# Two-layer attention and FFN trunk on one core: output projection accumulated head by head inside attention, probabilities scaled on the pool engine

## The reference

```python
# layer 0: 8 NSA heads, each with a compressed, a selected and a window branch, and 8 MLA heads
s = q @ k.T * scale + bias                 # per head and branch, causal
p = softmax(s)
o = gate_c * (p_c @ v_c) + gate_s * (p_s @ v_s) + gate_w * (p_w @ v_w)     # NSA
o = softmax(qn @ kn.T + qr @ kr.T) @ v                                      # MLA
x = x + gate * (concat(o, all 16 heads) @ w_out)                            # 2048 x 2048
# layer 1: 16 DSA heads, keys picked per token by an indexer's top 64
x = x + gate * (concat(o, 16 heads) @ w_out)
```

## Time and profile before

| what | value |
|---|---|
| median of 3 runs | 2169.94 us (2161.24 to 2180.1) |
| the profiled execution's own time | 2174.66 us |
| its span in the trace | 2173.0 us |
| its mean granted TensorE clock | 0.939 |
| busy PE, DVE, ACT, POOL | 1938.5, 1569.0, 1090.7, 129.2 us |

### The profile page before, as it was taken

How to read it: one execution, slowest core, us unless ns; L and a number is a source line. 1 busy time by engine, 2 the same in 40 slices (tenths; PEclk the granted TensorE clock), 3 DMA queues, 4 the chain that set the end, 5 groups by cost and what they waited for, 6 DMA issues and landing times.

```text
span 2173.0 us, 35788 instructions
## 1 busy us (share of the span) xinstructions
PE 1938.5 (89%) x11518; PEld 1684.7 (78%) x11518; DVE 1569.0 (72%) x2443; ACT 1090.7 (50%) x2384; POOL 129.2 (6%) x221
## 2 busy tenths in 40 slices
PE   3189978789899999999998999748989999999998
PEld 2068855567699999997777777636779999998787
DVE  4987743765787878887876767687766777778554
ACT  1145625674455455556454555346545555556443
POOL 1210000000100000000010000000000000000000
PEclk9589979799999999999999999669999999999999
DMA  8979965456588878785985998445757677665565
GB/s 326 401 258 342 328 232 161 155 174 216 172 284 272 278 245 280 255 278 188 327 281 187 331 314 308 137 163 203 251 182 226 221 242 223 221 221 171 178 188 178
DMA packets 210837, 521.47 MB, mean 240 GB/s; under 512 B 24945, under 2 KB 38770, under 8 KB 185874
## 3 DMA queue, kind: packets, MB, share of 16 engines
q1 hardware_dynamic: 180578, 316.17, 45.1%
q0 software_dynamic: 28032, 201.44, 25.1%
q10 hardware_dynamic: 2096, 2.12, 0.3%
HBM read 517.52 MB, written 2.12 MB: 239 GB/s over the span
## 4 chain that ended last, share of the span: by engine, by line
PE 77%; DVE 10%; DMA 6%; ACT 3%; issue 3%; SPq 0%; DVEq 0%; ACTq 0%; POOLq 0%
PE ps L794 12%; PE ps L789 12%; PE ps L790 12%; PE ps L860 11%; PE ps L856 11%; PE ps L857 11%; DVE acc L1381 4%; PE ps L916 2%; DMA first_ring<-in_ada_w 2%; PE ps L648 2%; DVE ring_lo L1449 1%; PE ps L908 1%; DMA ring<-in_ffn_w_down 1%; DMA ring<-in_od_w_in 1%; DMA ring<-in_ffn_w_up 1%
## 5 line engine op out<-in xcount | busy, mean ns | idle before, releaser
L1010 ACT ACTIVATE ring_hi<-ring 128x512 fp32r<-128x512 f32 (+1 forms) x1152 | 696.0, 622 | 657.4 <-DMA ring<-in_ffn_w_up 255.1
L1449 DVE TENSOR_TENSOR ring_lo<-ring,ring_hi 128x512 fp32r<-128x512 f32 (+1 forms) x1152 | 741.6, 679 | 373.4 <-ACT ring_hi L1010 371.5
L856 PE MATMUL ps<-hT_hi,ring_hi 128*128 128x256 f32 x2048 | 513.8, 283 | 5.3 <-issue 4.6
L857 PE MATMUL ps<-hT_lo,ring_hi 128*128 128x256 f32 x2048 | 508.7, 280 | 0.0
L856 PEld LDWEIGHTS ps<-hT_hi,ring_hi 128*128 128x128 f32 x2048 | 386.2, 189 | 6.1 <-issue 5.6
L857 PEld LDWEIGHTS ps<-hT_lo,ring_hi 128*128 128x128 f32 x2048 | 388.7, 190 | 0.0
L860 PE MATMUL ps<-hT_hi,ring_lo 128*128 128x256 f32 x2048 | 330.1, 282 | 1.5 <-issue 1.4
L789 PE MATMUL ps<-ring_hi,hT_hi 128*128 128x512 f32 (+2 forms) x768 | 302.0, 394 | 14.5 <-issue 9.4
L790 PE MATMUL ps<-ring_hi,hT_lo 128*128 128x512 f32 (+2 forms) x768 | 301.0, 393 | 0.0
L860 PEld LDWEIGHTS ps<-hT_hi,ring_lo 128*128 128x128 f32 x2048 | 280.1, 188 | 1.9 <-issue 1.6
L1381 DVE SCALAR_TENSOR_TENSOR acc<-aring,cs_now,acc 128x2048 f32<-128x2048 f32 x106 | 249.3, 2352 | 7.1 <-DMA aring<-in_ada_w 1.2
(11 more groups left out here) (205 smaller groups left out, 1662.6 us busy)
## 6 DMA issues: line engine op xcount, KB each, us to landing
aring<-in_ada_w POOLq DMA_DIRECT2D x176, 1024.0 KB, 6.4
ring<-in_ffn_w_up SPq DMA_DIRECT2D x512, 256.0 KB, 2.9
ring<-in_ffn_w_down SPq DMA_DIRECT2D x256, 256.0 KB, 3.2
ring<-in_od_w_in SPq DMA_DIRECT2D x128, 256.0 KB, 4.6
ring<-in_ev_w_in SPq DMA_DIRECT2D x96, 256.0 KB, 5.6
first_ring<-in_ada_w POOLq DMA_DIRECT2D x16, 1024.0 KB, 7.0
ring<-in_ev_w_out SPq DMA_DIRECT2D x64, 256.0 KB, 3.1
ring<-in_od_w_out SPq DMA_DIRECT2D x64, 256.0 KB, 3.2
```

The source lines that it names most:

```text
L856: nc.tensor.matmul(o[q], hi, hT_hi[:, kt, :], start=start, stop=False, skip_group_check=True)
L857: nc.tensor.matmul(o[q], hi, hT_lo[:, kt, :], start=False, stop=False, skip_group_check=True)
L1010: ins = nc.scalar.activation(out_, in_, f, **kw)
L1449: put(v.tensor_tensor(ring_lo[:, g, part], ring[:, g, part], ring_hi[:, g, part].bitcast(F32), ALU.subtract), lo_ok)
```

## The change

1. **Banks.** Attention has one bank each for logits, transposes, head output and queries (4 to 7). A bank is free again when its reader is done: `logits(n)` waits for DVE `logits(n-1)`, `values` of a new head waits for the end of the head before it. MLA's rotary part of the query (`rotary`) moves to the end of the iteration, since it shares the query bank.
2. **Products in attention.** Banks 0 to 3 hold column blocks 0 and 1 of the output. As soon as a head is finished, ACT rounds it from PSUM (`rounded`, one operation, written over the head's own query), DVE subtracts (`remainder`, instead of the copy to `hT`), and PE multiplies it with its two weight units (`product`, 12 matmuls of 512 columns), at iteration last + 5. ACT splits these two weight units at iteration last + 3, DVE at last + 4. SP fetches them in the order head, column block (`paired`).
3. **After attention** only column blocks 2 and 3 are left (`heads_out`), in banks 4, 5 and 0, 1; the gate is broadcast in two parts through banks 6 and 7. The pass that split hT, and the six units prepared ahead of attention, are gone.
4. **Scaling.** ACT `scale` is gone; POOL does the same two multiplications per unit, between its DMA loads of `ada_w`. DVE does `weights(n-1)` ahead of `logits(n)` instead of behind it.

The units left of the work for `c` are now spread over column block 2 alone: 5 of them in layer 0, 6 in layer 1.

```diff
+            def paired(name, w):
+
+                for kt in range(KT):
+                    for b in range(2):
+                        g = PLAN[name] + 2 * kt + b
+                        unit(g, g, w[kt * P:(kt + 1) * P, b * NB:(b + 1) * NB], ring[:, g % RING, :])
+                for b in range(2, 4):
+                    matrix(PLAN[name] + KT * b, w, KT, b * NB, NB)
...
+                    for m in range(len(att.units)):
+                        if m % 2 == 1 and rest:
+                            load(*rest.pop(0))
+                        pool.wait_ge(att.w_ok.handle, m + 1)
+                        for t, off, nk in ((1, 0, S), (0, S, P)):
...
+                            ins = nc.gpsimd.tensor_scalar(l, l, rw[:, m % 3, t:t + 1], None, ALU.mult)
+                        lane.done(ins, att.scaled)
...
-        S_B, T_B, O_B, Q_B = 0, 2, 4, 6
+        S_B, T_B, O_B, Q_B = 4, 5, 6, 7
...
-                if n >= 2:
-                    pe.wait_ge(att.l_ok.handle, n - 1)
+                if n >= 1:
+                    pe.wait_ge(att.l_ok.handle, n)
...
-                if first and q >= 2:
-                    pe.wait_ge(att.o_out.handle, q - 1)
+                if first and q >= 1:
+                    pe.wait_ge(att.o_out.handle, q)
...
+                rotary(n + 1)
+                q = head_at(att, n, PRODUCT_AT)
+                if q is not None:
+                    pe.wait_ge(att.o_out.handle, q + 1)
+                    for b in range(2):
+                        product(q, b)
...
+            def heads_out(name, n, att):
+
+                left = parts_of_heads(att)
+                pe_attention(pe, lane, att, head_product(name, left))
+                gate_rows(n, range(0, 2))
+                rows_block(name, 2 * KT, KT, NB, 4, left, part=(0, 6))
+                pe.wait_ge(gate_ok.handle, 4 * n + 2)
+                gate_rows(n, range(2, 4))
+                rows_block(name, 2 * KT, KT, NB, 4, left, part=(6, KT))
+                pe.wait_ge(gate_ok.handle, 4 * n + 4)
+                column_sums(n + 1)
+                pe.wait_ge(res_out.handle, 4 * n + 1)
+                rows_block(name, 3 * KT, KT, NB, 0, left, part=(0, 6))
+                column_turn(n + 1)
+                rows_block(name, 3 * KT, KT, NB, 0, left, part=(6, KT))
...
+            def heads_out(name, n, next_name):
+
+                highs(name, 2 * KT, 2 * KT + 4)
+                gate_copies(n, 1, range(0, 2))
+                highs(name, 2 * KT + 4, 2 * KT + 8)
+                gate_copies(n, 2, range(2, 4))
+                run(None, root[:, :], ones[:, 0:1], ACT.Sqrt)
+                highs(name, 2 * KT + 8, 2 * KT + 12)
...
-                for n in range(len(units) + 5):
+                for n in range(len(units) + LAG + 3):
+                    if 0 <= n - 1 < len(units):
+                        weights(n - 1)
                     if n < len(units):
                         logits(n)
-                    if 0 <= n - 1 < len(units):
-                        weights(n - 1)
-                    if 0 <= n - 4 < len(units):
-                        output(n - 4)
+                    remainder(n)
+                    q = head_at(att, n, SPLIT_AT + 1)
+                    if q is not None:
+                        lows(name, 2 * q, 2 * q + 2)
                     if n % every == every - 1:
                         rest_unit(n_sub)
```

More of the change, by code:

```diff
@@ L503, in trunk_program, with qheads @@
         CLEARED = (2, 5, 8, 11, 12)
+        CMP_REST, INDEX_REST = 3, 8
+        EV_UNITS = []
+        for h in range(NSA_H):
+            EV_UNITS += [("cmp", h), ("slc", h), ("win", h)]
+        EV_UNITS += [("mla", h) for h in range(MLA_H)]
+        OD_UNITS = [("dsa", h) for h in range(DSA_H)]
+        def qheads(units):
+            n, res, last = -1, [], None
+            for kind, h in units:
+                key = (kind == "mla", h)
+                if key != last:
+                    n, last = n + 1, key
+                res.append(n)
+            return res
@@ L505, in _, with head_at, kv_col @@
+        SPLIT_AT, PRODUCT_AT = 3, 5
+        def head_at(att, n, late):
+            return att.qh[n - late] if n - late in att.last_of else None
+        def kv_col(which, g):
+            return E_KV + (which * NSA_G + g) * HD
         @block.gpsimd
@@ L602, in pe_attention @@
+                for args in rest:
+                    load(*args)
+        def pe_attention(pe, lane, att, product):
             units, qh = att.units, att.qh
@@ L693, in pe_attention @@
             queries(0)
-            for n in range(len(units) + LAG + 1):
+            for n in range(len(units) + PRODUCT_AT):
                 queries(n + 1)
@@ L786, in rows_block @@
                         for t in range(ST):
-                            o, rows_ = ps[:, bank + t, 0:n], slice(t * P, (t + 1) * P)
-                            hi, lo = (part(u * UK + k)[:, rows_] for part in left)
+                            o = ps[:, bank + t, 0:n]
+                            hi, lo = (x(u * UK + k, t) for x in left)
                             nc.tensor.matmul(o, hi, w_hi[:, k, :], start=start, stop=False)
@@ L822, in out_side, with down @@
+            def down(name, n):
+                rows_block(name, 0, FT, NB, 0, act_parts, pairs_before=PAIRS_BEFORE[n, "out"])
+                pe.wait_ge(up_pair.handle, 32 * (n // 2 + 1))
                 gate_rows(n)
[L823 removed]
+                rows_block(name, FT, FT, NB, 2, act_parts)
                 for b in range(2):
@@ L1137, in out_side @@
-                for j in range(4):
-                    run(gate_ok, acc[:, 2, j * NB:(j + 1) * NB], ps[:, 4 + j, :], ACT.Copy)
+                gate_copies(n, 1)
                 if n < 3:
```

345 lines of the change are left out of this document (196 added, 149 removed).

## The result

| | before | after |
|---|---|---|
| median of the runs | 2169.59 us (8 runs) | 2183.32 us (8 runs, 2177.05 to 2196.08) |
| profiled execution, span | 2173.0 us | 2182.4 us |
| DVE busy | 72% | 71% |
| ACT busy | 50% | 49% |
| POOL busy | 6% | 9% |

The ratio to before is 1.007, 95% interval 1.004 to 1.0101. The forecast was 2156 us with a range to 2190: the time lies in the range, the direction is wrong.

The account below looks back on a forecast made before the run. The prediction took PE, busy 89%, as the bound, full in the out-projection but with room beside attention. Layer 0's terms gave -11.8 us and layer 1's -2.4, together -14: 2156 us on the median, range 2128 to 2190.

Parts of the forecast that it names:

- The failed step: Layer 0's 24 NSA units: six products hidden behind DVE, today's idle kept, 78 us against 69.9, +8.1 us.
- DVE has most of the work: NSA units: DVE busy 2.15 us of a 2.91 us period per unit, a chain of operations making the rest.
- My high bound for this part: NSA units: DVE's 59.9 us, today's idle 18.3 and six products of 2.77 us with none hidden, 94.8 us.
- 8 x 3.68: Layer 0's MLA part: PE bounds its eight units at 3.68 us each, before products and waits are added.
- The wait for the remainder: MLA units: values wait for DVE's remainder to free the single bank, PE stands 0.88 us in five iterations.
- The DSA iteration and its wait: Layer 1's DSA units: 2.30 us PE work, 2.77 product and 0.85 wait before values, 5.92 us.
- layer 1's attention: Layer 1's attention with drain: 97.1 us against 56.7, +40.4, the product time coming back almost whole.
- the rest of the out-projections: After attention: 52.0 and 52.7 us left, plus 3.5 and 4.5 us lost to ACT's and DVE's work.
- POOL's scaling: Scaling in attention: 1.2 us a unit, at most 1.8, hidden because PE wants the tile one iteration later.
- The stages overlap better: Rival, chance 0.27: NSA at its low end, no values wait, no loss after attention; 2124 us, half likelier, 2138.
- The scaling ends last: Rival, chance 0.12: POOL's scaling ends too late and lengthens iterations; 2201 us at 3.3 us a unit, deciding from 2.3.
- POOL and DVE hold each other up: Rival, chance 0.20: scaling that falls into DVE's unit for `c` ends after it; 10 us in NSA, 2166 us.

Follow-up runs that it names:

- thin_products: The changed kernel with the products of layer 0's heads 0 to 5 narrowed from 512 to 64 columns; 2176.33 us, ratio 1.0035.
- products_after: The changed kernel with ring operations and products of column blocks 0 and 1 done behind attention instead of inside it; 2213.64 us, ratio 1.0203.
- banks2_products_after: products_after with two banks again for logits, transposes and outputs; 2198.73 us, ratio 1.0106.
- spread_products: The changed kernel, each product's first half behind the next unit's logits, NSA heads' second half behind those one iteration later; 2156.37 us, ratio 0.9935.
- weights_behind: The changed kernel with DVE's weights behind the next logits again, as before; 2193.86 us, ratio 1.0105.
- pool_scale_only: The kernel before with only the scaling moved from ACT to POOL, DVE's order as before; 2203.53 us, ratio 1.0139.
- rest_apart: spread_products with the NSA part's twelve units for `c` in iterations where DVE has no remainder and no low operations; 2153.33 us, ratio 0.9915.

## Why the prediction was wrong, and where it was right

**The failed step** is in the NSA units: "I take today's idle and hide the products behind DVE: 78 us. The reason is that the product comes in the iteration after the one with the ring operations, in which PE runs ahead." PE does not run ahead there. With a single logits bank and the product at the iteration's end, the next logits stand behind the product, and DVE and ACT run dry (2.90 us in the row above). The row that the sum started from has PE busy 54.97 us and DVE 51.62; "DVE has most of the work" misreads it, and PE's 16.6 us of products were added to nothing. Of the 26.8 us that the part grew (97.0 against 70.2), thin_products gives 12.5 to PE's time for the columns and its difference to products_after 3.2 to the rest of the products and the ring operations. The other 11.1 are there without any product: 7.3 are the single banks (banks2_products_after), and what makes the last 3.8 is not separated; in that kernel PE waited 15.9 us for POOL, in before 14.9 for ACT at the same place. The small ones of these numbers are within what the clock moves. That the products cost this because of where they stand, and not because they are there, is shown by spread_products, which does the same work in the NSA part in 82.1 us; by how much through the clock is open.

My high bound for this part, 94.8 us, took the products as not hidden at all and was still 2.2 us too low, since it had no term for the banks and none for a unit at the low clock (2.68 us in the row, against 1.38; 22.9 us for the six products against 16.6).

**The second miss**, 6.2 us, is the term "8 x 3.68" of the MLA part. With a product an iteration is as forecast, 7.3 us; without one it is 5.0 to 5.6 instead of 3.68 (logits at 476.13, 481.73, 490.88, 495.89 and 501.19; the second of these four has a product). PE of after, first the logits of an iteration at the low clock level, then the starts of four iterations (the first two have no product) and one wait between:

```profile
481.73 1.06 PE L712 MATMUL ps<-knT,qT 128*128 128x256 f32 x2
...
490.44 0.38 PE L670 MATMUL ps<-con,side 128*128 128x128 f32 x2
...
495.43 0.41 PE L670 MATMUL ps<-con,side 128*128 128x128 f32 x2 [1.13 <-ACT qpT L1114]
...
499.02 0.49 PE L749 MATMUL ps<-PT,side 128*128 128x128 f32 x2 [0.59 <-DVE hT_lo L1765]
...
500.73 0.41 PE L670 MATMUL ps<-con,side 128*128 128x128 f32 x2 [0.56 <-ACT qpT L1114]
...
508.10 0.38 PE L670 MATMUL ps<-con,side 128*128 128x128 f32 x2
```

The wait for `qpT`, the rotary half that goes through the one queries' bank, is in no term of the prediction. The diff shows it, and I did not price it; where a product stands behind the rotary transposes it is hidden. The wait for the remainder was priced only beside products, and it is there without one too (0.59 us in the row). Three iterations without a product were 4.9 us over their 3 x 3.68 together; 3.4 of that are these two waits (qpT 0.56, 1.13 and 0.56, remainder 2 x 0.59). The first one with a product took 9.15 instead of 7.3 (logits at 481.73 and at 490.88), and it started at the lower clock level: its first logits matmuls took 1.06 us, those at 490.88 0.60.

**Right.** The DSA iteration and its wait (by the prediction's own terms 1.26 - 0.46 = 0.80, not 0.85); layer 1's attention (98.55 against 97.1), where the products' time came back whole; the rest of the out-projections (56.6 and 59.1 against 55.5 and 57.2), in which PE's largest waits are 3.3 us for DVE's low part in layer 0 and 2.9 for a unit for `c` in layer 1, as priced.

**POOL's scaling.** Mis-sized (1.80 us a unit, forecast 1.2) and hidden, as forecast. The reason is not that POOL is fast enough, though. With the weights behind the logits PE waits 15.5 us for it (weights_behind), and with two banks and no products 15.9 (banks2_products_after), against 0.2 in after: it is hidden by the weights ahead of the logits and by the slower pipeline around it. Put alone into before, it costs 1.4%.

**The rivals.** "The stages overlap better" was wrong of this kernel and right of the possibility: with the products in other places the kernel comes to 2156 us, by chance the number that was forecast, but for other reasons, and at a clock of 0.85 in the NSA part, as that rival had it rise. (Half of its 32 us is 2140, not 2138.) "The scaling ends last", which was to decide from 2.3 us a unit on, decides in pool_scale_only, where the unit takes 1.34 + 1.09 = 2.43 us (groups by form), and does not in after with 1.80. "POOL and DVE hold each other up" is seen in the same place; in after PE waits 0.2 us for POOL. None of the rivals had the case that came: that PE's product holds up the loop that DVE and ACT live on.

**A version that beats both** is spread_products, 2156.37 us, 0.9935 of before (0.9909 to 0.9962), and rest_apart, 2153.33 us, 0.9915 (0.988 to 0.995), which is not told apart from it. From the first attention logits to the first FFN matmul, layer 0 takes 222.7 us before, 237.5 after and 221.1 in spread_products; layer 1 takes 167.5, 168.8 and 155.2. So nearly all of the gain over before is layer 1's, and of the 17.9 us between these two profiled executions another 6.0 lie between the two stretches, where nothing was changed.

## What to carry to other kernels

When work is moved into a loop that goes round several engines, ask what stands behind it on its own engine. In this kernel it came nearly free only where the other engines had just been given their next work, directly behind the matmuls that feed them, and in halves of 1.5 us; whole products there, or a half left at the iteration's end, were not hidden. Free time in a windows row (PE busy 55.0 of 69.9 us) is no room by itself, a clock of 0.76 in it means that added matmuls may cost nearly twice their price at full clock (2.68 us against 1.38), and a buffer given up for the change (here a second bank) is a cost of its own, to be priced before the gain. Such an order is cheap to try in two or three variants, and here the variants differ by more than the change itself.

## What the runs showed of the hardware

- POOL's tensor_scalar in float32 takes as mean 973 ns for 256 elements and 831 for 128 beside DVE's work. A pair of both without a neighbour took 1.51 us:

```profile
433.27 1.51 POOL L648 TENSOR_SCALAR L<-L,rw 128x256 f32<-128x256 f32 x2
```

- Beside DVE's unit for `c` (two inputs from SBUF, 2.35 us) the operation of 256 elements alone took 3.07 us, about the 2.35 more, while DVE's took what it always takes. The Trainium skill, "SBUF — State Buffer", section Who interferes with whom, calls the port pair that VectorE and GpSimd share an exclusive lock, and lets a VectorE instruction with two SBUF inputs contend with a GpSimd one that reads SBUF; the row agrees. It says too that issue order decides which of the two blocks; the rows start 0.01 us apart, POOL's first, and it is POOL that waited, which neither bears this out nor refutes it, since starts on POOL can't be read so finely.
- The same matmuls cost PE 78.91 us at a granted clock of 0.76 and 67.09 at 0.85, and only the products' places in PE's stream differed. In products_after, with 72 fewer of them, the clock was 0.69. The MLA stretch, with the same code and the same waits, had 1.00 in one kernel and 0.92 in another, and took 56.5 and 60.8 us.
